# A weight sum moved from VectorE to an adding DMA issued by GpSimd, in a decoder layer's feed-forward units

## Chip, cores and metric

The kernel runs on one core of one Trainium2 chip. The metric is the device time of one execution in microseconds, as the median of several runs. Engines are named as in the profile: PE is TensorE (PEld its weight loads), DVE is VectorE, ACT is ScalarE, POOL is GpSimd, SP is SyncE, which here only issues DMAs.

## What is computed

One layer of a decoder in float32: 256 tokens (SEQ), model width 2048, feed-forward width 5504 (D_FF). The change touches the two feed-forward networks only.

```python
def swiglu_ffn(x, w_in, w_out):
    gate, up = jnp.split(x @ w_in, 2, axis=-1)
    return (jax.nn.silu(gate) * up) @ w_out

x = x + 0.5 * swiglu_ffn(rmsnorm(x, ffn1_norm[l]), ffn1_w_in[l], ffn1_w_out[l])
h = rmsnorm(x, mix_norm[l])
...   # attention mixer of two head groups, then x = x + mixed @ w_out
x = x + 0.5 * swiglu_ffn(rmsnorm(x, ffn2_norm[l]), ffn2_w_in[l], ffn2_w_out[l])
```

## The kernel before

**Products in three parts.** Every float32 operand is split into a high part (ACT copies it to float32r, tile `whi`) and a low part (DVE subtracts the high part from the original, tile `wlo`); a product is hi x hi + hi x lo + lo x hi on TensorE. The weights are split in "halves" of 128 x 1024 elements. `whi` and `wlo` have four slots, so ACT may split half h only when TensorE has used half h - 4 (`weights_used`), and TensorE takes half h when DVE has made its low part (`weights_lo`). `split` is L671 on ACT and L951 on DVE.

**Units.** `x @ w_in` is computed in 11 units of 512 columns of gate and up (`UNITS`, the last has 384). Unit 0 is plain. Units 1 to 10 compute part of the product by a scheme of Strassen's kind with seven products in place of eight: besides plain blocks of the weights (B11, B21, B22 and the plain quarters G0, G1, U0, U1) it multiplies four sums of weight blocks, T1 to T4, with four sums of activation blocks (`form_sums`) or a plain one. A unit uses 22 halves in the order T1, B11, G0, T2, B21, T3, G1, B22, T4, U (four halves: the two of U0, the two of U1), where the halves of G and U need twelve matmuls each and the others six. A "quarter of U" below is one such half.

**Sums.** DVE makes the sums of 128 x 2048 elements: T1 = B12 - B11 into the tile `tsum` (L1042), T3 = B22 - B12 in the slot of B12 (L1049), T2 = T3 + B11 in the slot of B11 (L1056) and T4 = B21 - T2 into `tsum` (L1062). Each of the sums is written out by hand at a fixed place between DVE's splits; engines work through their instructions strictly in this order. T1 and T3 of the next unit are made in the last two quarters of U of this one.

**Loads.** Each unit reads eight pieces of 1 MB from HBM into six slots of the tile `raw`. SP issues them in the order B11, B12, B22, G0, B21, G1, U0, U1; piece n takes the slot of piece n - 6 and waits until that is free (`free`), and all later pieces wait behind it. So U0 waits for the slot of B11 (which holds T2), U1 for that of B12 (T3), the next unit's B11 for that of B22, its B12 for G0's, and its B22 for B21's. Before the change the slot of B11 is free when the T4 sum is done:

```python
if i == LOAD["B11"]:
    return sums_done, 4 * ((UNITS - 1) * u + j)
last = {LOAD["B21"]: B21, LOAD["B12"]: T3, LOAD["B22"]: B22, ...
```

**GpSimd** makes a few small powers and issues the small loads: in the first network's time `bias_vector` and its copy to 128 rows of 12 KB in HBM, `bias_vectors` (L340, L342), then, once `weights_lo` has reached `OUT[0]`, the constants of the mixer.

**After the units** the product with `w_out` follows, with its own pieces, and, between the two networks, the mixer. They are as before in both kernels.

Of the kernel before, what the change touches and what calls it, by code (L numbers as in the profile page):

```python
# [91 lines left out]
def layer(nc, io, out):  # L92
# [3 lines left out]
    with ctx:  # L96
# [110 lines left out]
        def act_slot(u, c, p):  # L207
# [11 lines left out]
        silu_done, act_f_done, act_psum, act_copied, aw_hi_ready, aw_ready = (  # L219
            sem(n) for n in ("silu_done", "act_f_done", "act_psum", "act_copied", "aw_hi_ready", "aw_ready"))  # L220
        xg_ready, s_summed, s_hi, s_ready = (sem(n) for n in ("xg_ready", "s_summed", "s_hi", "s_ready"))
        sums_done, copied, w_done, gate_added, c11_done = (
            sem(n) for n in ("sums_done", "copied", "w_done", "gate_added", "c11_done"))
        sq_done, hss_ready, hms_ready, hr_ready, hsc_ready, qn_ready, qk_psum, qkT_ready, v_ready = (
# [13 lines left out]
        def _(sp):  # L238
            def free(n):
                for u in range(2):  # L240
                    if IN_P[u] <= n < OUT_P[u]:
                        j, i = (n - IN_P[u]) // 8, (n - IN_P[u]) % 8
                        if j == 0:
                            return weights_lo, IN[u] + 2 * i + 2
                        if i == LOAD["B11"]:
                            return sums_done, 4 * ((UNITS - 1) * u + j)
                        last = {LOAD["B21"]: B21, LOAD["B12"]: T3, LOAD["B22"]: B22, LOAD["G0"]: G0, LOAD["G1"]: G1, LOAD["U0"]: U0, LOAD["U1"]: U0 + 2}[i]
                        return weights_lo, unit_half(u, j) + last + 2
                    end = (QKV_P, END_P)[u]
                    if OUT_P[u] <= n < end:  # L250
                        c, q = (n - OUT_P[u]) // ACT_PAIRS, (n - OUT_P[u]) % ACT_PAIRS
                        return weights_lo, OUT[u] + FT * c + min(2 * q + 2, FT)
                return weights_lo, QKV + 2 * (n - QKV_P) + 2
# [63 lines left out]
        @block.gpsimd  # L317
        def _(pool):
            pool.memset(neg_half[:], -0.5).then_inc(small_set, 1)
            pool.memset(warm[:], 0.0).then_inc(small_set, 1)  # L320
            pool.memset(ident[:], 0.0).then_inc(ident_zero, 1)
            pool.wait_ge(ident_zero, 1)
            pool.affine_select(out=ident[:], in_=ident[:], compare_op=ALU.not_equal, fill=1.0, base=0,
                               pattern=[[-1, P]], channel_multiplier=1).then_inc(ident_ready, 1)
            pool.dma_start(table[:], io["rel_bias_table"]).then_inc(vec_loaded, 16)
            pool.dma_start(one_hot[:], io["c_one_hot"]).then_inc(vec_loaded, 16)
            pool.dma_start(vec_mask[:], io["c_vec_mask"]).then_inc(vec_loaded, 16)
            for s, name in enumerate(("mix_norm", "ffn2_norm")):
                pool.dma_start(gain_rows2[s * KT:(s + 1) * KT, :], io[name][0].rearrange("(k p) -> k p", p=P)).then_inc(gains2_loaded, 16)
            for s, name in enumerate(("q_norm_a", "k_norm_a", "q_norm_b", "k_norm_b")):  # L330
                pool.dma_start(gain_rows2[2 * KT + s:2 * KT + s + 1, :], io[name]).then_inc(gains2_loaded, 16)

            def x_power(s):
                pool.wait_ge(xms_ready, s + 1)
                pool.tensor_tensor(rstd[:, s, :], xms[:, s, :], neg_half[:, 0:TB], ALU.pow).then_inc(rstd_ready, 1)

            pool.wait_ge(small_set, 2)
            x_power(0)
            pool.wait_ge(vec_ready, 1)
            pool.dma_start(vec_dram.rearrange("a (h v) -> (a h) v", h=H_A), vec[:]).then_inc(vec_stored, 16)  # L340
            pool.wait_ge(vec_stored, 16)
            pool.dma_start(scratch, vec_dram.to_broadcast([P, H_A * VEC])).then_inc(vec_copied, 16)  # L342
            pool.wait_ge(weights_lo, OUT[0])
            pool.dma_start(wf[:], io["w_in"][0].rearrange("(k p) f -> p k f", p=P)[:, :, 6 * D_A:6 * D_A + H_B]).then_inc(f_loaded, 16)
            pool.dma_start(f_bias[:], io["forget_bias"].to_broadcast([P, H_B])).then_inc(f_loaded, 16)
            pool.dma_start(mult[:], io["c_mult"]).then_inc(mixer_loaded, 16)
            pool.dma_start(causal[:], io["c_causal"]).then_inc(mixer_loaded, 16)
            pool.dma_start(upper[:], io["c_upper"]).then_inc(mixer_loaded, 16)
            pool.wait_ge(weights_lo, QKV)
            pool.wait_ge(vec_copied, 16)  # L350
            for b in range(TB):
                src = bass.AP(tensor=scratch.tensor, offset=SEQ - 1 - b * P,
                              ap=[[H_A * VEC - 1, P], [VEC, H_A], [1, (b + 1) * P]])
                pool.dma_start(dmat[:, 0:H_A, b * P:b * P + (b + 1) * P], src).then_inc(mixer_loaded, 16)
            x_power(1)
            for m in range(2 * GROUPS):
                pool.wait_ge(hms_ready, m + 1)
                pool.tensor_tensor(hr[:], hms[:], neg_half[:].rearrange("p (b i) -> p b i", b=TB), ALU.pow).then_inc(hr_ready, 1)
            x_power(2)

        @block.tensor
        def _(pe):
# [299 lines left out]
        def _(act_e):  # L662
# [102 lines left out]
            def unit(u, j):  # L765
                Y, V, Z, X = unit_banks(j)
                base, n, w, s = unit_half(u, j), IN_P[u] + 8 * j, UNIT_W[j], j % 2
                first, w2 = (UNITS - 1) * u + j - 1, 2 * w
                act_e.wait_ge(sums_done, 4 * first + 1)
                for i in range(2):  # L770
                    split(base + T1 + i, tsum[:, i * w2:(i + 1) * w2], w2)
                loaded(n + LOAD["B11"])
# [7 lines left out]
                act_e.wait_ge(weights_used, base + B11 + 2)  # L780
                act_e.wait_ge(act_f_done, 2 * (UNITS * u + j))
                A(p1s[:, 0:w], Y[:, 0:w], ACT.Copy).then_inc(copied, 1)
                act_e.wait_ge(sums_done, 4 * first + 3)
                for i in range(2):
                    split(base + T2 + i, piece_half(n + LOAD["B11"], i, w2), w2)
                loaded(n + LOAD["B21"])
# [10 lines left out]
                for i in range(2):  # L797
                    split(base + B22 + i, piece_half(n + LOAD["B22"], i, w2), w2)
                act_copy(u, j - 1)
                act_e.wait_ge(sums_done, 4 * first + 4)  # L800
                for i in range(2):
                    split(base + T4 + i, tsum[:, i * w2:(i + 1) * w2], w2)
                loaded(n + LOAD["U0"])
                for i in range(2):
                    split(base + U0 + i, piece_half(n + LOAD["U0"], i, w2), w2)
# [140 lines left out]
        def _(dve):  # L946
# [24 lines left out]
            def form_sums(u):  # L971
# [1 line left out]
                A11, A21, A12, A22 = xg[:, 0:4, 0:P], xg[:, 0:4, P:2 * P], xg[:, 4:8, 0:P], xg[:, 4:8, P:2 * P]  # L973
                V.tensor_tensor(A22, A21, A22, ALU.add).then_inc(s_summed, 1)
                dve.wait_ge(s_summed, 4 * u + 1)
                V.tensor_tensor(A21, A11, A21, ALU.subtract).then_inc(s_summed, 1)
                V.tensor_tensor(A11, A22, A11, ALU.subtract).then_inc(s_summed, 1)
                dve.wait_ge(s_summed, 4 * u + 3)
                V.tensor_tensor(A12, A12, A11, ALU.subtract).then_inc(s_summed, 1)

            def form_splits(u):
                for f in range(4):
# [53 lines left out]
            def sum_t1(u, j):  # L1036
# [1 line left out]
                full(n + LOAD["B11"])  # L1038
                full(n + LOAD["B12"])
                if j > 1:  # L1040
                    dve.wait_ge(weights_lo, unit_half(u, j - 1) + T4 + 2)
                V.tensor_tensor(tsum[:, 0:4 * w], whole(n + LOAD["B12"], w), whole(n + LOAD["B11"], w),  # L1042
                                ALU.subtract).then_inc(sums_done, 1)

            def sum_t3(u, j):
                n, w = IN_P[u] + 8 * j, UNIT_W[j]
                full(n + LOAD["B22"])
                dve.wait_ge(sums_done, 4 * ((UNITS - 1) * u + j - 1) + 1)
                V.tensor_tensor(whole(n + LOAD["B12"], w), whole(n + LOAD["B22"], w), whole(n + LOAD["B12"], w),  # L1049
                                ALU.subtract).then_inc(sums_done, 1)  # L1050

            def sum_t2(u, j):
                n, w = IN_P[u] + 8 * j, UNIT_W[j]
                dve.wait_ge(sums_done, 4 * ((UNITS - 1) * u + j - 1) + 2)
                dve.wait_ge(weights_lo, unit_half(u, j) + B11 + 2)
                V.tensor_tensor(whole(n + LOAD["B11"], w), whole(n + LOAD["B12"], w), whole(n + LOAD["B11"], w),  # L1056
                                ALU.add).then_inc(sums_done, 1)

            def sum_t4(u, j):
                n, w = IN_P[u] + 8 * j, UNIT_W[j]  # L1060
                dve.wait_ge(sums_done, 4 * ((UNITS - 1) * u + j - 1) + 3)
                V.tensor_tensor(tsum[:, 0:4 * w], whole(n + LOAD["B21"], w), whole(n + LOAD["B11"], w),  # L1062
                                ALU.subtract).then_inc(sums_done, 1)

            def plain_unit(u):
# [25 lines left out]
            def unit(u, j):  # L1091
# [11 lines left out]
                for i in range(2):  # L1103
                    split(base + T2 + i, piece_half(n + LOAD["B11"], i, w2), w2)
                split(base + B21, piece_half(n + LOAD["B21"], 0, w2), w2)
                sum_t4(u, j)
                split(base + B21 + 1, piece_half(n + LOAD["B21"], 1, w2), w2)
                for i in range(2):
                    split(base + T3 + i, piece_half(n + LOAD["B12"], i, w2), w2)
# [4 lines left out]
                V.tensor_tensor(gset[:, s, 1, 0:w], Y[:, 0:w], gset[:, s, 1, 0:w], ALU.add).then_inc(w_done, 1)  # L1114
                for i in range(2):
                    split(base + B22 + i, piece_half(n + LOAD["B22"], i, w2), w2)
                split(base + T4, tsum[:, 0:w2], w2)
                dve.wait_ge(weights_used, base + G1 + 2)
                dve.wait_ge(w_done, first + 1)
                V.tensor_tensor(gset[:, s, 1, 0:w], X[:, 0:w], gset[:, s, 1, 0:w], ALU.add).then_inc(gate_added, 1)  # L1120
                split(base + T4 + 1, tsum[:, w2:2 * w2], w2)
                split(base + U0, piece_half(n + LOAD["U0"], 0, w2), w2)
                dve.wait_ge(weights_used, base + B22 + 2)
                dve.wait_ge(copied, 3 * first + 3)
# [208 lines left out]
```

## Time and profile before

| | before |
|---|---|
| median of 3 runs | 1793.67 us (1792.72 to 1793.70) |
| the profiled execution | 1793.74 us, its span 1791.9 us |
| granted TensorE clock, mean | 1.000 |
| PE busy | 1785.4 us |
| DVE busy | 1330.9 us |
| ACT busy | 1015.1 us |
| POOL busy | 28.6 us |
| DMA | 347.14 MB, mean 194 GB/s |

The profile is of one execution. Times in it are microseconds from the start of the span; the execution's own time is 1.8 us longer than its span. "Busy" counts an engine's instructions without waits, and matmuls overlap: one row says 0.39 us, while the next starts 0.23 us later. A line number names the line of the kernel that issued an instruction; L671 and L951 are the shared helper `split`. A load's "us to landing" runs from its issue to its semaphore.

### The profile page before, as it was taken

Reading aid. Unit: us, or ns where it says so; the run is one execution under the profiler, and the core shown is the slowest. Engines: PE = TensorE matmul, PEld = TensorE weight load, DVE = VectorE, ACT = ScalarE, POOL = GpSimd, SP = SyncE. Lnnn points to the kernel's source line nnn. Section 1 sums busy time; section 2 is a strip of 40 time slices with the busy share of each in tenths; the row PEclk is TensorE's granted clock in tenths of the full one; section 3 lists DMA queues with packets and bytes.
Section 4 is the critical chain, followed back from the end, with each engine's and each line's share of the span. In section 5 each row is a group of like instructions: output and inputs, shape, how many; then the busy total and the mean of one; then the engine's idle time right before and its main releaser. Section 6 shows DMA issues by size and latency. Waiting matters only on the chain.

```text
span 1791.9 us, 20728 instructions
## 1 busy us (share of the span) xinstructions
PE 1785.4 (100%) x8196; PEld 1491.0 (83%) x8196; DVE 1330.9 (74%) x1389; ACT 1015.1 (57%) x1244; POOL 28.6 (2%) x37
## 2 busy tenths in 40 slices
PE   9999999999999999999999999999999999999999
PEld 7888888888888888888888888888888888988887
DVE  6999999998755655565655655999999998855654
ACT  6666666666644544544545544666666666644543
POOL 1000000000000000000000000000000000000000
PEclk9999999999999999999999999999999999999999
DMA  8555555554855554445455456355555554655761
GB/s 330 189 214 218 213 188 188 188 188 167 297 196 191 187 176 176 157 149 184 154 179 164 167 185 252 126 210 191 214 217 216 216 214 154 246 189 182 229 193 53
DMA packets 153663, 347.14 MB, mean 194 GB/s; under 512 B 5840, under 2 KB 14096, under 8 KB 153440
## 3 DMA queue, kind: packets, MB, share of 16 engines
q1 hardware_dynamic: 151536, 340.28, 54.5%
q0 software_dynamic: 1168, 3.97, 0.6%
q10 hardware_dynamic: 864, 1.58, 0.2%
q8 instruction: 65, 1.06, 0.2%
q14 instruction: 30, 0.25, 0.0%
HBM read 343.70 MB, written 3.68 MB: 194 GB/s over the span
## 4 chain that ended last, share of the span: by engine, by line
PE 99%; DVE 0%; DMA 0%; ACT 0%; issue 0%; ACTq 0%; DVEq 0%
PE bank L434 10%; PE bank L436 10%; PE bank L435 10%; PE bank L500 9%; PE bank L499 9%; PE bank L501 9%; PE bank L422 7%; PE bank L424 7%; PE bank L423 7%; PE bank L372 6%; PE bank L374 6%; PE bank L373 6%; PE bank L404 1%; PE bank L393 1%; PE bank L529 0%; PE bank L576 0%
## 5 line engine op out<-in xcount | busy, mean ns | idle before, releaser
L951 DVE TENSOR_TENSOR wlo<-raw,whi 128x1024 fp32r<-128x1024 f32 (+1 forms) x692 | 824.5, 1209 | 377.7 <-ACT whi L671 373.5
L671 ACT ACTIVATE whi<-raw 128x1024 fp32r<-128x1024 f32 (+1 forms) x692 | 721.1, 1048 | 613.9 <-PE bank L501 224.3
L434 PE MATMUL bank<-whi,xs 128*128 128x512 f32 (+1 forms) x768 | 297.7, 388 | 0.3 <-DVE wlo L951 0.3
L436 PE MATMUL bank<-whi,xs 128*128 128x512 f32 (+1 forms) x768 | 295.6, 385 | 0.0
L435 PE MATMUL bank<-wlo,xs 128*128 128x512 f32 (+1 forms) x768 | 295.4, 385 | 0.0
L499 PE MATMUL bank<-whi,aw_hi 128*128 128x512 f32 x676 | 263.4, 390 | 0.0
L501 PE MATMUL bank<-whi,aw_lo 128*128 128x512 f32 x676 | 263.1, 389 | 0.0
L500 PE MATMUL bank<-wlo,aw_hi 128*128 128x512 f32 x676 | 263.0, 389 | 0.0
L434 PEld LDWEIGHTS bank<-whi,xs 128*128 128x128 f32 x768 | 144.2, 188 | 27.7 <-issue 1.2
L436 PEld LDWEIGHTS bank<-whi,xs 128*128 128x128 f32 x768 | 144.2, 188 | 27.7
L435 PEld LDWEIGHTS bank<-wlo,xs 128*128 128x128 f32 x768 | 144.3, 188 | 26.7
L372 PE MATMUL bank<-whi,xs 128*128 128x512 f32 x384 | 156.1, 406 | 0.0
L374 PE MATMUL bank<-whi,xs 128*128 128x512 f32 x384 | 150.2, 391 | 0.0
L373 PE MATMUL bank<-wlo,xs 128*128 128x512 f32 x384 | 149.7, 390 | 0.0
L501 PEld LDWEIGHTS bank<-whi,aw_lo 128*128 128x128 f32 x676 | 126.9, 188 | 26.4
L499 PEld LDWEIGHTS bank<-whi,aw_hi 128*128 128x128 f32 x676 | 126.9, 188 | 26.2
L500 PEld LDWEIGHTS bank<-wlo,aw_hi 128*128 128x128 f32 x676 | 126.9, 188 | 26.1
L671 ACT ACTIVATE whi<-tsum 128x1024 fp32r<-128x1024 f32 (+1 forms) x80 | 83.0, 1040 | 96.5 <-PE bank L436 63.8
L422 PE MATMUL bank<-whi,sf 128*128 128x512 f32 (+1 forms) x320 | 122.8, 384 | 0.0
L424 PE MATMUL bank<-whi,sf 128*128 128x512 f32 (+1 forms) x320 | 122.8, 384 | 0.0
L423 PE MATMUL bank<-wlo,sf 128*128 128x512 f32 (+1 forms) x320 | 122.8, 384 | 0.0
L951 DVE TENSOR_TENSOR wlo<-tsum,whi 128x1024 fp32r<-128x1024 f32 (+1 forms) x80 | 94.0, 1197 | 25.7 <-ACT whi L671 25.7
(168 smaller groups left out, 1973.5 us busy)
## 6 DMA issues: line engine op xcount, KB each, us to landing
raw<-ffn_w_in SPq DMA_DIRECT2D x159, 1024.0 KB, 7.1
raw<-ffn_w_out SPq DMA_DIRECT2D x84, 1024.0 KB, 5.5
raw<-w_in SPq DMA_DIRECT2D x48, 1024.0 KB, 5.0
raw<-w_out SPq DMA_DIRECT2D x16, 1024.0 KB, 4.9
raw<-ffn_w_in SPq DMA_DIRECT2D x16, 768.0 KB, 4.5
x<-x SPq DMA_DIRECT2D x4, 512.0 KB, 8.9
raw<-ffn_w_out SPq DMA_DIRECT2D x4, 512.0 KB, 3.8
bias_vectors<-bias_vector POOLq DMA_DIRECT2D x1, 1536.0 KB, 9.3
```

The costliest lines, as they stand in the source:

```text
L372: mm(banks[b][:, 0:w], stationary[:, k, 0, tok], hi, start=k == 0, stop=False, skip_group_check=True)
L373: mm(banks[b][:, 0:w], stationary[:, k, 0, tok], lo, start=False, stop=False, skip_group_check=True)
L374: last = mm(banks[b][:, 0:w], stationary[:, k, 1, tok], hi, start=False, stop=k == k_total - 1, skip_group_check=True)
L422: mm(bank_out[:, 0:w], st_hi, hi, start=start and i == 0 and k == 0, stop=False, skip_group_check=True)
L434: mm(banks[b][:, 0:w], xs[:, k + i, 0, tok], hi, start=starts[b] and k + i == 0, stop=False, skip_group_check=True)
L435: mm(banks[b][:, 0:w], xs[:, k + i, 0, tok], lo, start=False, stop=False, skip_group_check=True)
L436: last = mm(banks[b][:, 0:w], xs[:, k + i, 1, tok], hi, start=False, stop=k + i == last_k, skip_group_check=True)
L499: mm(banks[i][b][:], st_hi, hi, start=k == 0, stop=False, skip_group_check=True)
L500: mm(banks[i][b][:], st_hi, lo, start=False, stop=False, skip_group_check=True)
L501: last = mm(banks[i][b][:], st_lo, hi, start=False, stop=k == FT - 1, skip_group_check=True)
L671: A(whi[:, h % SLOTS, 0:n_el], src, ACT.Copy).then_inc(weights_hi, 1)
L951: V.tensor_tensor(wlo[:, h % SLOTS, 0:n_el], src, whi[:, h % SLOTS, 0:n_el].bitcast(f32), ALU.subtract).then_inc(weights_lo, 1)
```

## The change

In units 1 to 10 of both networks VectorE's T4 sum is gone. GpSimd issues a DMA with `accum_op=ALU.add` from the slot of B11, which holds T2, into the slot of B21, which so becomes T4. It waits for the T2 sum and for the low part of B21. A DMA can add and not subtract, so the signs of T2 and T3 are turned (and in `form_sums` those of the activation sums multiplied with them). The slot of B11 becomes free when this transfer has landed, the slot of B21 after the split of T4, and the sum of the next T1 into `tsum` waits only for the split of T1.

```diff
@@ loads (SP)
                         if i == LOAD["B11"]:
-                            return sums_done, 4 * ((UNITS - 1) * u + j)
-                        last = {LOAD["B21"]: B21, ...
+                            return t4_summed, 16 * ((UNITS - 1) * u + j)
+                        last = {LOAD["B21"]: T4, ...
@@ GpSimd
+            def sum_t4(u, j):
+                n, w, first = IN_P[u] + 8 * j, UNIT_W[j], (UNITS - 1) * u + j - 1
+                b11, b21 = raw_slot(n + LOAD["B11"]), raw_slot(n + LOAD["B21"])
+                pool.wait_ge(sums_done, 3 * first + 3)
+                pool.wait_ge(weights_lo, unit_half(u, j) + B21 + 2)
+                pool.dma_start(raw[:, b21, 0:4 * w], raw[:, b11, 0:4 * w], accum_op=ALU.add).then_inc(t4_summed, 16)
+
+            for j in range(1, UNITS):
+                sum_t4(0, j)
             pool.wait_ge(weights_lo, OUT[0])
...
             x_power(2)
+            for j in range(1, UNITS):
+                sum_t4(1, j)
@@ ScalarE, unit
-                act_e.wait_ge(sums_done, 4 * first + 4)
-                for i in range(2):
-                    split(base + T4 + i, tsum[:, i * w2:(i + 1) * w2], w2)
+                act_e.wait_ge(t4_summed, 16 * (first + 1))
+                for i in range(2):
+                    split(base + T4 + i, piece_half(n + LOAD["B21"], i, w2), w2)
@@ VectorE, form_sums
-                V.tensor_tensor(A21, A11, A21, ALU.subtract).then_inc(s_summed, 1)
-                V.tensor_tensor(A11, A22, A11, ALU.subtract).then_inc(s_summed, 1)
+                V.tensor_tensor(A21, A21, A11, ALU.subtract).then_inc(s_summed, 1)
+                V.tensor_tensor(A11, A11, A22, ALU.subtract).then_inc(s_summed, 1)
                 dve.wait_ge(s_summed, 4 * u + 3)
-                V.tensor_tensor(A12, A12, A11, ALU.subtract).then_inc(s_summed, 1)
+                V.tensor_tensor(A12, A12, A11, ALU.add).then_inc(s_summed, 1)
@@ VectorE, sum_t1, sum_t3, sum_t2
-                    dve.wait_ge(weights_lo, unit_half(u, j - 1) + T4 + 2)
+                    dve.wait_ge(weights_lo, unit_half(u, j - 1) + T1 + 2)
...
-                V.tensor_tensor(whole(n + LOAD["B12"], w), whole(n + LOAD["B22"], w), whole(n + LOAD["B12"], w),
+                V.tensor_tensor(whole(n + LOAD["B12"], w), whole(n + LOAD["B12"], w), whole(n + LOAD["B22"], w),
                                 ALU.subtract).then_inc(sums_done, 1)
...
                 V.tensor_tensor(whole(n + LOAD["B11"], w), whole(n + LOAD["B12"], w), whole(n + LOAD["B11"], w),
-                                ALU.add).then_inc(sums_done, 1)
-
-            def sum_t4(u, j):
-                n, w = IN_P[u] + 8 * j, UNIT_W[j]
-                dve.wait_ge(sums_done, 4 * ((UNITS - 1) * u + j - 1) + 3)
-                V.tensor_tensor(tsum[:, 0:4 * w], whole(n + LOAD["B21"], w), whole(n + LOAD["B11"], w),
                                 ALU.subtract).then_inc(sums_done, 1)
@@ VectorE, unit
                 split(base + B21, piece_half(n + LOAD["B21"], 0, w2), w2)
-                sum_t4(u, j)
                 split(base + B21 + 1, piece_half(n + LOAD["B21"], 1, w2), w2)
...
-                split(base + T4, tsum[:, 0:w2], w2)
+                split(base + T4, piece_half(n + LOAD["B21"], 0, w2), w2)
...
-                split(base + T4 + 1, tsum[:, w2:2 * w2], w2)
+                split(base + T4 + 1, piece_half(n + LOAD["B21"], 1, w2), w2)
```

`sums_done` now counts three sums a unit, and the waits on it are renumbered.

## Rows read from the trace of the kernel before

**Rows 1.** The page's first part: busy time, share of the span, instructions.
```profile
PE 1785.4 (100%) x8196; PEld 1491.0 (83%) x8196; DVE 1330.9 (74%) x1389; ACT 1015.1 (57%) x1244; POOL 28.6 (2%) x37
```

**Rows 2.** Busy time by stretches; then granted clock, DMA share, GB/s.
```profile
1189.00:1550.00 361.00, 361.00 (x1667) 304.20 (x1666) 330.94 (x285) 233.94 (x261) 0.00 (x0) 1.00 0.54 195
...
262.60:304.30 41.70, 41.70 (x189) 34.61 (x188) 38.41 (x33) 26.80 (x29) 0.00 (x0) 1.00 0.55 200
273.00:280.60 7.60, 7.60 (x36) 6.27 (x35) 7.46 (x7) 4.67 (x5) 0.00 (x0) 1.00 0.00 0
```

**Rows 3.** Instructions of DVE in order: start, us, line, operation, count, idle before.
```profile
278.28 2.28 DVE L1062 TENSOR_TENSOR tsum<-raw 128x2048 f32<-128x2048 f32 x1
280.48 2.36 DVE L951 TENSOR_TENSOR wlo<-raw,whi 128x1024 fp32r<-128x1024 f32 x2
...
293.40 1.23 DVE L951 TENSOR_TENSOR wlo<-tsum,whi 128x1024 fp32r<-128x1024 f32 x1 [0.40 <-ACT whi L671]
...
298.98 2.28 DVE L1042 TENSOR_TENSOR tsum<-raw 128x2048 f32<-128x2048 f32 x1
301.18 1.22 DVE L951 TENSOR_TENSOR wlo<-raw,whi 128x1024 fp32r<-128x1024 f32 x1
...
307.06 1.22 DVE L951 TENSOR_TENSOR wlo<-raw,whi 128x1024 fp32r<-128x1024 f32 x1 [0.19 <-ACT whi L671]
308.62 0.75 DVE L1004 SCALAR_TENSOR_TENSOR gset<-bank,rstd,gset 128x512 f32<-128x512 f32 x1 [0.34 <-PE bank L436]
...
310.68 2.35 DVE L951 TENSOR_TENSOR wlo<-raw,whi 128x1024 fp32r<-128x1024 f32 x2
```

**Rows 4.** PE's first matmul of T4, of U, of B11's second half (next unit).
```profile
294.82 0.39 PE L422 MATMUL bank<-whi,xs 128*128 128x512 f32 x1
...
297.54 0.39 PE L434 MATMUL bank<-whi,xs 128*128 128x512 f32 x1
...
312.50 0.39 PE L422 MATMUL bank<-whi,xs 128*128 128x512 f32 x1
```

**Rows 5.** The T4 sums of DVE: duration in ns min/median/max, forms.
```profile
L1062 DVE TENSOR_TENSOR tsum<-raw x20: 1753/2284/2289, 69.7 to 1530.6; 128x2048 f32<-128x2048 f32 x18, 128x1536 f32<-128x1536 f32 x2
```

**Rows 6.** ACT in order: high part of B21's second half, of T4, of U0.
```profile
278.70 1.06 ACT L671 ACTIVATE whi<-raw 128x1024 fp32r<-128x1024 f32 x1 [1.60 <-PE bank L436]
...
289.64 1.06 ACT L671 ACTIVATE whi<-tsum 128x1024 fp32r<-128x1024 f32 x1 [0.75 <-PE bank L436]
...
293.72 1.06 ACT L671 ACTIVATE whi<-raw 128x1024 fp32r<-128x1024 f32 x1 [0.36 <-PE bank L424]
```

**Rows 7.** SP's waits for the T4 sum: us in total, times, longest.
```profile
SPq L261 <- DVE tsum L1062: 389.8, 20, 20.6
```

**Rows 8.** Loads and landing: U0 alone; B11', B12', B22' together.
```profile
L261 SPq DMA_DIRECT2D raw<-ffn_w_in x1: 368/368/368, 280.6 to 280.6; - x1
...
DMA to landing us min/median/max: 5.0/5.0/5.0
...
L261 SPq DMA_DIRECT2D raw<-ffn_w_in x2: 367/437/507, 289.9 to 290.3; - x2
...
L261 SPq DMA_DIRECT2D raw<-ffn_w_in x3: 367/505/507, 289.9 to 290.8; - x3
...
DMA to landing us min/median/max: 5.0/7.2/9.2
```

**Rows 9.** DMA issues of GpSimd: KB each, us to landing.
```profile
dmat<-bias_vectors POOLq DMA_DIRECT2D x1, 1024.0 KB, 9.8
...
bias_vector<-vec POOLq DMA_DIRECT2D x1, 12.0 KB, 1.7
```

**Rows 10.** The 128-row transfer's issue; queues in 52 to 55.2, then from 55.2.
```profile
52.03 0.55 POOL L342 DMA_DIRECT2D bias_vectors<-bias_vector  x1 [1.46 <-DMA bias_vector<-vec]
...
q1 hardware_dynamic: 479, 0.98, 92.4%
...
q0 software_dynamic: 144, 1.57, 74.5%
```

More of the change, by code:

```diff
@@ L221, in layer @@
         xg_ready, s_summed, s_hi, s_ready = (sem(n) for n in ("xg_ready", "s_summed", "s_hi", "s_ready"))
+        t4_summed = sem("t4_summed")
         sums_done, copied, w_done, gate_added, c11_done = (
@@ L245, in free @@
                         if i == LOAD["B11"]:
-                            return sums_done, 4 * ((UNITS - 1) * u + j)
-                        last = {LOAD["B21"]: B21, LOAD["B12"]: T3, LOAD["B22"]: B22, LOAD["G0"]: G0, LOAD["G1"]: G1, LOAD["U0"]: U0, LOAD["U1"]: U0 + 2}[i]
+                            return t4_summed, 16 * ((UNITS - 1) * u + j)
+                        last = {LOAD["B21"]: T4, LOAD["B12"]: T3, LOAD["B22"]: B22, LOAD["G0"]: G0, LOAD["G1"]: G1, LOAD["U0"]: U0, LOAD["U1"]: U0 + 2}[i]
                         return weights_lo, unit_half(u, j) + last + 2
@@ L768, in unit @@
                 first, w2 = (UNITS - 1) * u + j - 1, 2 * w
-                act_e.wait_ge(sums_done, 4 * first + 1)
+                act_e.wait_ge(sums_done, 3 * first + 1)
                 for i in range(2):
@@ L782, in unit @@
                 A(p1s[:, 0:w], Y[:, 0:w], ACT.Copy).then_inc(copied, 1)
-                act_e.wait_ge(sums_done, 4 * first + 3)
+                act_e.wait_ge(sums_done, 3 * first + 3)
                 for i in range(2):
@@ L1047, in sum_t3 @@
                 full(n + LOAD["B22"])
-                dve.wait_ge(sums_done, 4 * ((UNITS - 1) * u + j - 1) + 1)
-                V.tensor_tensor(whole(n + LOAD["B12"], w), whole(n + LOAD["B22"], w), whole(n + LOAD["B12"], w),
+                dve.wait_ge(sums_done, 3 * ((UNITS - 1) * u + j - 1) + 1)
+                V.tensor_tensor(whole(n + LOAD["B12"], w), whole(n + LOAD["B12"], w), whole(n + LOAD["B22"], w),
                                 ALU.subtract).then_inc(sums_done, 1)
@@ L1053, in sum_t2 @@
                 n, w = IN_P[u] + 8 * j, UNIT_W[j]
-                dve.wait_ge(sums_done, 4 * ((UNITS - 1) * u + j - 1) + 2)
+                dve.wait_ge(sums_done, 3 * ((UNITS - 1) * u + j - 1) + 2)
                 dve.wait_ge(weights_lo, unit_half(u, j) + B11 + 2)
                 V.tensor_tensor(whole(n + LOAD["B11"], w), whole(n + LOAD["B12"], w), whole(n + LOAD["B11"], w),
-                                ALU.add).then_inc(sums_done, 1)
-            def sum_t4(u, j):
-                n, w = IN_P[u] + 8 * j, UNIT_W[j]
-                dve.wait_ge(sums_done, 4 * ((UNITS - 1) * u + j - 1) + 3)
-                V.tensor_tensor(tsum[:, 0:4 * w], whole(n + LOAD["B21"], w), whole(n + LOAD["B11"], w),
                                 ALU.subtract).then_inc(sums_done, 1)
```

## The prediction

> **What bounds the kernel now.** I read the page's first part, then the table by stretches, then one unit of the first feed-forward layer instruction by instruction on every engine. The first part [rows 1] shows TensorE busy 1785.4 of 1791.9 us, VectorE 74%, GpSimd 2%. By stretches [rows 2] TensorE is busy 361.0 of 361.0 us where the units of the second layer lie and 41.70 of 41.70 in the unit under study, at full clock. So nothing taken off VectorE inside the units can shorten the kernel; what can happen there is that TensorE starts to wait.
>
> A unit lasts 41.7 us [rows 2]. The matmul rows [rows 4] give the deadlines of the unit under study: T4 is needed at 294.82, the first quarter of U at 297.54. T4's 12 matmuls took 2.72 us, and each quarter of U has 12: so the last one is needed at 297.54 + 3 x 2.72 = 305.70, and the second half of the next unit's B11 at 312.50. ("Next" things carry a prime below.) On DVE, from the T1' sum at 298.98 on, one instruction follows the next with only two small waits, 0.19 and 0.34 us, up to the low part of the second half of B11', which starts at 310.68, takes 1.22 us (first of two), and so ends at 311.90 [rows 3]. TensorE wants it at 312.50: 0.60 us to spare. That is the narrowest place I found. DVE may therefore be late at the T1' sum by 0.19 + 0.34 + 0.60 = 1.13 us before TensorE waits.
>
> **The change part by part.**
>
> *Removed: the VectorE sums.* 20 of them, 18 of 2.284 us and the two of the narrow last units 1.753 us [rows 5], 44.6 us in all. They are hidden behind TensorE, so this gives 0. In the unit, DVE does the sum from 278.28 to 280.56 and then the low part of the second half of B21, from 280.48 [rows 3]; ACT delivers that half's high part at 278.70 + 1.06 = 279.76, held by TensorE [rows 6]. So with the sum gone that low part ends near 279.8 + 1.23 = 281.03 instead of 281.7: a start of the new work only 0.7 us earlier than before.
>
> *Turned signs.* The same subtractions and additions at the same shapes; 0. The T1' sum now waits only for T1's split, long past; 0.
>
> *Added: 20 adding transfers of 1 MB on GpSimd's queue.* GpSimd waits for the T2 sum (five instructions before the T4 sum on DVE, long done) and for the low part of B21, so it issues at 281.06. Queued behind it on GpSimd in layer 1 are five constant loads that wait for the end of the units anyway, and in layer 2 nothing: 0. When it issues, nothing is in flight: the data engines moved 0 GB/s from 273.0 to 280.6 [rows 2], and the loads behind it are the very ones that wait for it. Call D its time from issue to landing. No adding transfer stands in the trace, so I bound D.
> Below: a plain 1 MB load issued by SP with the engines idle lands in 5.0 us [rows 8]; loads queued one behind another land 2.6 and 2.5 us apart (289.9 + 5.0 = 294.9, 290.3 + 7.2 = 297.5, 290.8 + 9.2 = 300.0) [rows 8], so 2.55 us is data and 2.4 us fixed.
> GpSimd's queue starts later: of the transfer of 128 rows of 12 KB issued at 52.03 [rows 10] no packet had moved by 55.2, when only SP's queue appears, and in the window from 55.2 on it is there [rows 10]: 3.2 us. With data at copy speed D would be 3.2 + 2.55 = 5.75.
> But an adding transfer has to read both the T2 slot and the B21 slot for each result, and I take the reads as the limit: 2 x 2.55 = 5.1. D = 3.2 + 5.1 = 8.3, and 0.2 for the completion, which the rows don't separate: 8.5 us. I take this value, since it is nearest to a row in kind (same queue, 128 rows). Above: the 1 MB gather-like load of the mixer on this queue landed in 9.8 us among other traffic [rows 9]; and if the adder runs at half the pace of the doubled reads, 3.2 + 10.2 = 13.4.
>
> The Trainium skill, Collectives: The Full Stack, in "Why ReduceScatter is half of AllGather", says that an add in the data engines costs no cycles of its own and halves the rate only because two sources are read. By that rule the sum would be the one made here with 8.5 (1828 us), without it that of 13.4 (1906 us, below). No row of this trace shows an add, so it stays unconfirmed.
>
> *What hangs on D: the T4 split.* ACT takes T4 at 289.64 [rows 6]; TensorE needs it at 294.82, less 1.06 + 1.23 for the two parts: until 292.5. From 281.06 that is D = 11.4. At 8.5 it costs 0.
>
> *The slot of B11.* It was free when the T4 sum ended (280.56) and U0's load was issued at once, at 280.6; SP spent 389.8 us in 20 waits for exactly this [rows 7]. Now U0's load waits for the landing: issue at I = 281.06 + D + 0.03. It lands at I + 5.0 = 294.6 for D = 8.5; ACT wants it at 293.72, but TensorE only needs the low part by 297.54, so it may land until 295.2 (D = 9.1). Costs 0 by itself.
>
> *What is late next.* This is the term that decides. Behind U0 SP's queue holds U1, B11', B12'. Before, U0 and U1 were out of the way when B11' was issued at 289.9 with the engines free; B12' landed at 297.5 and the T1' sum, which needs it, started at 298.98 [rows 3, 8]. Now U0's load is issued at 289.59 and four loads run one after the other: B12' lands at I + 5.0 + 3 x 2.55 = I + 12.65 = 302.2. The T1' sum starts then: 302.2 - 298.98 = 3.3 us late. Behind it on DVE stand the last quarter of U (ends at 302.40 + 3.3 = 305.7, needed at 305.70: just), the T3' sum, T1', B11'. 3.26 less the 1.13 of slack is 2.1 us of TensorE waiting, in general 281.09 + D + 12.65 - 298.98 - 1.13 = D - 6.4 us.
> All later times of the unit that are tied to TensorE move by the same 2.1 us, the next adding transfer too, since DVE, freed of its sum, regains its lateness before B21 (1.4 us of room: B21's first half ended at 278.36, 279.76 is held by TensorE [rows 3, 6]). So it recurs and neither grows nor heals.
>
> *The slot of B21.* It now frees after T4's second low part, 293.40 + 1.23 = 294.63 [rows 3], instead of at 281.7, so B22' and all behind it on SP's queue can't be issued before that; before it was issued at 290.8 [rows 8]. With the engines idle it would land at 299.7, and behind B12' it lands at 304.8; the T3' sum wanted it at 302.3, behind the split of 301.18 [rows 3], and wants it at 305.6 in the forecast. Costs 0 either way; the cover is DVE's own lateness, 0.8 us of it.
>
> *How often.* Each layer has ten such units; the last has no successor with sums, and the ninth's successor has 384 columns: its two loads are 0.64 us shorter each, its two sums 0.53 each, its splits together an estimated 0.8, against 1.0 us by which its deadline is nearer; that is 2.1 us less 1.28 + 1.06 + 0.8 - 1.0 = 2.1, so nothing. So 8 per layer, 16 in all: 16 x 2.1 = 34 us.
>
> **Sum.** The profiled execution took 1793.74 us (its span 1791.9, 1.8 around it), 0.07 above the median of the runs: 1793.7 + 34 = 1828 us.
>
> **The rivals.**
> *Quick start.* The 12 KB transfer on the same queue landed in 1.7 us [rows 9]. If 128 rows start as fast, D = 1.7 + 5.1 = 6.8, the wait is 0.4 a unit, 7 us in all: 1801. For it: the 3.2 us come from one transfer amid traffic. Against: that one has 16 times the rows.
> The Trainium skill, DMA: Bandwidth & Descriptors, section "Anatomy of one DMA — SWDGE (gpsimd) path", puts a transfer on this queue at 2.0 us plus its bytes at 436 GB/s; with bytes read twice that is an estimate of 6.8, where the first-packet delay in this trace speaks for more.
> *Hidden anyway.* At copy speed D is 5.75, or 5.0 as on SP's queue; both are under 6.4, TensorE never waits: 1794. For it: everything else in the unit has room. Against: two reads.
> *Adder slow.* D = 13.4: the wait is 7.0 a unit through the same chain (the T4 and U0 deadlines are passed as well, by 2.0 and 4.3 us, but they lie on the same chain and don't add): 16 x 7.0 = 112, so 1906. For it: no row shows what the adder does. Against: nothing but that the reads alone explain a cost.
> *Faster.* Its one mechanism: VectorE's 44.6 us less lets a wait of TensorE's inside the units vanish. It decides only if there is one; the unit under study and the second layer's stretch show none. If the rest of the 6.5 us idle [rows 1] had such waits, all of it at most: 1787. A transfer that lands early changes nothing on TensorE.
> That the change doesn't do what it says is not open: one form of T4 or the other must feed the matmuls.
>
> **How the numbers follow.** D between 7.5 and 10 (forecast, 1811 to 1852): 0.43. D from 6.6 to 7.5 (quick start): 0.12. D above 10: 0.24, half of it above 12. D below 6.6, no change: 0.18. Faster: 0.03. 0.2%, 3.6 us, is about what these runs can tell from nothing; it is 0.2 us a unit, D = 6.6. So slower 0.79, same 0.18, faster 0.03. The range runs from 1793 (no change) to D = 12, 16 x 5.6 = 90: 1884; it leaves out 0.12 above and 0.03 below. The forecast's own range is 1811 to 1852.
>
> **What would show it.** The adding transfer's time to landing near 8.5 us; SP's wait for U0's slot near 28 us each; DVE idle some 3.3 us before most T1 sums, ended by a load; TensorE waiting some 2 us before the second half of B11 and nowhere else, at a unit period near 43.8; VectorE's busy time down by 44.6. I'm wrong if D is under 6.4, if loads run behind one another faster than 2.55 us, if TensorE waits at T4 or U0 instead, or if the wait heals in the next unit.

## The result and the profile after

The changed kernel took 1825.67 us (median, 1824.61 to 1826.41), the kernel before 1793.68 us in the same session: ratio 1.0178, 95% interval 1.0165 to 1.0191, 32 us slower. The forecast was 1828, its own range 1811 to 1852. Two single executions of kernels below were in a slow state (4302.60 us with the two half transfers, 2235.94 with the load held less) and are left out of the medians given.

First the page's first part, then the table by stretches (columns: busy us and count for PE, PEld, DVE, ACT, POOL; granted clock, DMA share, GB/s), which answer to [rows 1, 2]:

```profile
span 1822.8 us, 20748 instructions
PE 1795.1 (98%) x8196; PEld 1487.5 (82%) x8196; DVE 1288.3 (71%) x1369; ACT 1011.3 (55%) x1244; POOL 45.8 (3%) x57
```
```profile
70.00:450.00 380.00, 366.90 (x1621) 296.78 (x1620) 310.54 (x266) 229.90 (x252) 7.77 (x9) 1.00 0.63 217
1190.00:1540.00 350.00, 342.79 (x1532) 281.17 (x1531) 295.46 (x254) 216.71 (x236) 6.82 (x8) 1.00 0.64 224
```

VectorE's busy time fell by 42.6 us (forecast 44.6; its other rows together took 2.0 longer) and TensorE gained idle time where it had none: 13.1 us in 380 of layer 1, 7.2 in 350 of layer 2, still at full clock. (That is less than the time lost: around a wait TensorE's rows overlap less and read longer, 0.47 and 0.50 us below against 0.39, so PE's busy total rose by 9.7 us as well.)

DVE in the unit that corresponds to [rows 3], in order:

```profile
293.42 2.59 DVE L964 TENSOR_TENSOR wlo<-raw,whi 128x1024 fp32r<-128x1024 f32 x2 [1.23 <-ACT whi L684]
...
316.07 2.29 DVE L1055 TENSOR_TENSOR tsum<-raw 128x2048 f32<-128x2048 f32 x1 [3.40 <-DMA raw<-ffn_w_in]
318.28 1.22 DVE L964 TENSOR_TENSOR wlo<-raw,whi 128x1024 fp32r<-128x1024 f32 x1
...
325.02 0.74 DVE L1017 SCALAR_TENSOR_TENSOR gset<-bank,rstd,gset 128x512 f32<-128x512 f32 x1
...
327.07 2.35 DVE L964 TENSOR_TENSOR wlo<-raw,whi 128x1024 fp32r<-128x1024 f32 x2
```

The second half of B21 is split from 293.42 on, held by ScalarE as forecast, and its low part ends at 294.64. The T1' sum (now L1055) then waits 3.40 us for a load, where nothing waited before; the two small waits that followed it have vanished (no bracket at 325.02). Between this low part and the T1' sum lies the new work. GpSimd's row in order of time, then the time from issue to landing of this one transfer:

```profile
295.18 0.85 POOL L350 DMA_DIRECT2D raw<-raw  x1 [43.52 <-DVE wlo L964]
```
```profile
DMA to landing us min/median/max: 6.8/6.8/6.8
```

SP's loads U0 and U1, issued together, and B12' (duration of the issue in ns, first and last start; then us to landing):

```profile
L262 SPq DMA_DIRECT2D raw<-ffn_w_in x2: 368/438/508, 302.0 to 302.5; - x2
DMA to landing us min/median/max: 4.9/6.0/7.0
...
L262 SPq DMA_DIRECT2D raw<-ffn_w_in x1: 627/627/627, 303.9 to 303.9; - x1
DMA to landing us min/median/max: 12.1/12.1/12.1
```

GpSimd issues at 295.18 and the transfer lands 6.8 us later, at 302.0. At that moment SP issues U0, then U1, and B12' as the fourth at 303.9: it lands at 303.9 + 12.1 = 316.0, and the T1' sum starts at 316.07. SP's waits and TensorE's own rows of the same unit (start, us, line, idle before):

```profile
SPq L262 <- DMA raw<-raw: 528.0, 20, 30.2
```
```profile
322.98 0.47 PE L435 MATMUL bank<-whi,sf 128*128 128x512 f32 x1 [0.40 <-DVE wlo L964]
...
328.34 0.50 PE L435 MATMUL bank<-whi,xs 128*128 128x512 f32 x1 [1.00 <-DVE wlo L964]
```

SP's 20 waits for the slot of B11 grew from 19.5 us each [rows 7] to 26.4 (forecast: near 28), and TensorE waits at T1' and at the second half of B11'.

The two layers don't pay alike. GpSimd's power ahead of layer 2's units marks the border; it began at 1133.15 in the kernel before, and here:

```profile
1153.27 1.60 POOL L336 TENSOR_TENSOR rstd<-xms,neg_half 128x2 f32<-128x2 f32 x1 [145.47 <-DVE xms L1003]
```

So layer 1 pays 20.1 us and layer 2 the rest of the 30.9 us by which the span grew, 10.8. The border of each kernel below is this same row. Compared matmul by matmul with the kernel before, TensorE falls further behind in eight units of each layer, by 2.5 us a unit on average in layer 1 and 1.3 in layer 2, and not in the ninth (the last costs 0.5 in layer 2).

### The profile page after: what moved, and what is told of

It is laid out like the page before. It is cut to its first block, busy times and chain, and to the rows that moved or that the text cites. A ratio compares the mean times of both kernels' runs of the same rounds, so it can differ in the third digit from the quotient of the medians.

```text
span 1822.8 us, 20748 instructions
## 1 busy us (share of the span) xinstructions
PE 1795.1 (98%) x8196; PEld 1487.5 (82%) x8196; DVE 1288.3 (71%) x1369; ACT 1011.3 (55%) x1244; POOL 45.8 (3%) x57
## 3 DMA queue, kind: packets, MB, share of 16 engines
q8 instruction: 65, 1.06, 0.2%
## 4 chain that ended last, share of the span: by engine, by line
PE 73%; DVE 12%; DMA 10%; issue 4%; ACT 0%; SPq 0%; DVEq 0%; POOLq 0%; ACTq 0%
PE bank L513 8%; PE bank L514 8%; PE bank L512 8%; DMA raw<-ffn_w_in 8%; PE bank L385 6%; PE bank L387 6%; PE bank L386 6%; DVE wlo L964 6%; PE bank L447 5%; PE bank L449 5%; PE bank L448 5%; PE bank L435 4%; PE bank L437 3%; PE bank L436 3%; DVE tsum L1055 2%
## 5 line engine op out<-in xcount | busy, mean ns | idle before, releaser
L964 DVE TENSOR_TENSOR wlo<-raw,whi 128x1024 fp32r<-128x1024 f32 (+1 forms) x732 | 872.7, 1208 | 437.0 <-ACT whi L684 432.3
L684 ACT ACTIVATE whi<-raw 128x1024 fp32r<-128x1024 f32 (+1 forms) x732 | 761.3, 1047 | 643.2 <-PE bank L514 224.4
L447 PE MATMUL bank<-whi,xs 128*128 128x512 f32 (+1 forms) x768 | 298.8, 389 | 3.4 <-DVE wlo L964 3.2
L449 PE MATMUL bank<-whi,xs 128*128 128x512 f32 (+1 forms) x768 | 295.6, 385 | 0.0
L448 PE MATMUL bank<-wlo,xs 128*128 128x512 f32 (+1 forms) x768 | 295.4, 385 | 0.0
L435 PE MATMUL bank<-whi,xs 128*128 128x512 f32 (+1 forms) x240 | 94.2, 392 | 14.9 <-DVE wlo L964 14.9
L436 PE MATMUL bank<-wlo,xs 128*128 128x512 f32 (+1 forms) x240 | 92.2, 384 | 0.0
```

The source lines that it names most:

```text
L435: mm(bank_out[:, 0:w], st_hi, hi, start=start and i == 0 and k == 0, stop=False, skip_group_check=True)
L436: mm(bank_out[:, 0:w], st_hi, lo, start=False, stop=False, skip_group_check=True)
L447: mm(banks[b][:, 0:w], xs[:, k + i, 0, tok], hi, start=starts[b] and k + i == 0, stop=False, skip_group_check=True)
L448: mm(banks[b][:, 0:w], xs[:, k + i, 0, tok], lo, start=False, stop=False, skip_group_check=True)
L449: last = mm(banks[b][:, 0:w], xs[:, k + i, 1, tok], hi, start=False, stop=k + i == last_k, skip_group_check=True)
L684: A(whi[:, h % SLOTS, 0:n_el], src, ACT.Copy).then_inc(weights_hi, 1)
```

## The experiments

**The slot of B11 freed early.** The adding transfer stays, but T2 is written into `tsum`, which is free since T1's split, and the slot of B11 is free when that sum is done. The next T1 sum waits for the transfer instead.

```diff
-                            return t4_summed, 16 * ((UNITS - 1) * u + j)
+                            return sums_done, 3 * ((UNITS - 1) * u + j)
...
-                pool.dma_start(raw[:, b21, 0:4 * w], raw[:, b11, 0:4 * w], accum_op=ALU.add).then_inc(t4_summed, 16)
+                pool.dma_start(raw[:, b21, 0:4 * w], tsum[:, 0:4 * w], accum_op=ALU.add).then_inc(t4_summed, 16)
...
-                    dve.wait_ge(weights_lo, unit_half(u, j - 1) + T1 + 2)
+                    dve.wait_ge(t4_summed, 16 * ((UNITS - 1) * u + j - 1))
...
-                V.tensor_tensor(whole(n + LOAD["B11"], w), whole(n + LOAD["B12"], w), whole(n + LOAD["B11"], w),
+                V.tensor_tensor(tsum[:, 0:4 * w], whole(n + LOAD["B12"], w), whole(n + LOAD["B11"], w),
```
(T2's splits on both engines read `tsum`.)

> The adding transfer stays, but T2 is made in tsum, so the slot of B11 is free when the T2 sum is done (near 273.5 in the unit of the profile before) and U0's load no longer waits for the transfer. Theory A (the cost is the row U0, U1, B11', B12' on SP's queue behind the landing, which delays the T1' sum): B12' lands as before, 1794 us, within 3. Rival B (the late slot of B21, which holds B22' and all behind it): unchanged by this edit, 1826. Rival C (the transfer itself: its traffic, or T4 arriving late at ScalarE): 1826 as well.

Measured: 1793.62 us, ratio 1.0000 (0.9990 to 1.0009). Its page, then the landing of its 20 transfers:

```profile
span 1791.9 us, 20748 instructions
PE 1785.4 (100%) x8196; PEld 1490.9 (83%) x8196; DVE 1290.9 (72%) x1369; ACT 1015.4 (57%) x1244; POOL 45.9 (3%) x57
```
```profile
DMA to landing us min/median/max: 6.7/7.9/9.1
```

The transfers are there (and even slower, 7.9 us in the median, beside loads), the slot of B21 is as late as in the change, the signs are turned, 20 sums are gone from VectorE: all of that together costs and gives nothing. The cost of the change hangs on how late the slot of B11 is freed.

**Two transfers of half the size.**

```diff
-                pool.wait_ge(weights_lo, unit_half(u, j) + B21 + 2)
-                pool.dma_start(raw[:, b21, 0:4 * w], raw[:, b11, 0:4 * w], accum_op=ALU.add).then_inc(t4_summed, 16)
+                for i in range(2):
+                    c = slice(2 * w * i, 2 * w * (i + 1))
+                    pool.wait_ge(weights_lo, unit_half(u, j) + B21 + 1 + i)
+                    pool.dma_start(raw[:, b21, c], raw[:, b11, c], accum_op=ALU.add).then_inc(t4_summed, 16)
```

> The transfer is cut in two of 512 KB, each issued when its half of B21 is split. The second has half the data, 2.5 us in place of 5.1, so U0's load is issued some 2.5 us earlier, near 285.6 in the clock of the unit before. Theory A: threshold for that is about 287.1, so no wait is left or a few tenths where a data engine is held up: 1794 to 1800 us. Rival B: 1826. Rival C with a cost per transfer: over 1826.

Measured: 1795.86 us, ratio 1.0012 (1.0003 to 1.0022). Each half landed in 4.5 us (median) in place of 6.9; the loss is gone but for 2.1 us.

**A plain copy in place of the add.**

```diff
-pool.dma_start(raw[:, b21, 0:4 * w], raw[:, b11, 0:4 * w], accum_op=ALU.add)
+pool.dma_start(raw[:, b21, 0:4 * w], raw[:, b11, 0:4 * w])
```

> The same transfer as a plain copy of T2 over B21; the addition is left out. If the doubled reads are the reason for the transfer's 6.9 us, it lands in 6.9 - 2.5 = 4.4 us, and by theory A TensorE hardly waits: 1794 to 1800 us. If the add itself were costless or the time came from GpSimd's queue, it would still land in 6.9 and the time stay 1826. Rival B: 1826.

Measured: 1794.01 us, ratio 1.0003 (0.9993 to 1.0012). The DMA issues (KB each, us to landing), of the changed kernel and then of this one:

```profile
raw<-raw POOLq DMA_DIRECT2D x18, 1024.0 KB, 6.9
```
```profile
raw<-raw POOLq DMA_DIRECT2D x18, 1024.0 KB, 4.5
```

The add costs 2.4 us over the copy, about one more pass of 1 MB at 2.55 us [rows 8]: what I had charged for reading two sources. (No run tells the second read from the addition itself.)

**The kernel before, with U0's load held.** No adding transfer at all.

```diff
-                            return sums_done, 4 * ((UNITS - 1) * u + j)
+                            return weights_lo, unit_half(u, j) + B22 + 1
```

> The kernel before, with VectorE's T4 sum and no adding transfer, but U0's load held until the low part of B22's first half is done (288.7 in the unit of the profile before, where the change puts its issue near 288.5). Theory A: the same waits as with the change, 1.2 to 2.5 us a unit, 1815 to 1830 us. Rivals B and C (slot of B21, traffic, T4 late): none of them is there, 1794.

Measured: 1824.57 us, ratio 1.0173 (1.0156 to 1.0190), the change's time within 1.1 us; layer 1 pays 17.0 and layer 2 13.6 us. The late load alone is enough for the whole loss.

**The same, held 2.2 us less** (`G1 + 2` in place of `B22 + 1`).

> The kernel before with U0's load held until the low part of G1's second half is done, 286.5 in the unit of its profile. Theory A with its threshold near 286.7 to 287.1: 1794 to 1799 us, against 1824.6 when held until 288.7. If holding U0's load costs something at any length: well over 1800.

Measured: 1795.09 us, ratio 1.0008 (0.9998 to 1.0018). 2.2 us of delay separate 1.4 us of loss from 30.9: there is a threshold. By an estimate from these two, 29.5 us over 16 units are 1.8 us a unit, which puts it near 286.9, between the two releases (286.5 and 288.7, as times of the unit in the profile before).

**The transfer one half later.**

```diff
-                pool.wait_ge(weights_lo, unit_half(u, j) + B21 + 2)
+                pool.wait_ge(weights_lo, unit_half(u, j) + B21 + 3)
```

> The adding transfer waits for one more low part (first half of T3), 1.36 us later. Theory A says that every microsecond of delay is one of waiting in 16 to 18 units: 1826 + 22 = 1848 us, plus or minus 4. If the T4 split or the slot of B21 set the wait, the delay would be taken up by their slack (over 2 us before T4 is wanted): 1826.

Measured: 1849.68 us, 24.0 over the changed kernel; layer 1 pays 12.0 us more, layer 2 13.1. In total that is one for one in 18 units (18 x 1.36 = 24.5). Unit by unit it is uneven: from one adding transfer to the next, layer 1's units grew by 0.2 to 2.5 us over those of the change.

**Half of U1's load left out.**

```diff
-                        piece(n + LOAD["U1"], w_in[:, 4:8, up], 4, w)
+                        piece(n + LOAD["U1"], w_in[:, 4:6, up], 2, w)
```

> The changed kernel with U1's load cut to half its bytes; the second half of that piece is left out and stale data are used. Theory A: four loads run in a row from the landing to B12', each 2.57 us; with 1.28 us less, B12' lands that much earlier and each of 16 to 18 waits shrinks by 1.1 to 1.3 us: 1826 - 20 = 1806 us, plus or minus 3. If U0's own lateness or the T4 split made TensorE wait: 1826.

Measured: 1801.14 us. A load that nobody was late for (U1), made shorter, takes back 24.5 of 32 us: the waits belong to the row of loads. It is 2 us beyond the expected margin. Layer 1 gained 14.7 us, of which 1.0 lies ahead of the units (the first power row stands at 43.42 in place of 44.39), so 13.7 in eight units, 1.7 each, more than the 1.3 us of load; layer 2 gained 7.6. The excess lies in every second unit of layer 1, which gained 1.8 to 2.4 us, the others 1.2 to 1.4. In the change's second unit B12' landed 14.0 us after the adding transfer had, and a 16 KB block of instructions fell into its last stretch, 18.4 us after that transfer's issue (such blocks are the subject further down). With the shorter load the block comes 18.4 us after the issue again, but B12' has already landed, at 18.3 and 11.3 us after the adding transfer.

**VectorE's sum in the slot of B21.** The signs and slots of the change, but the sum is VectorE's, after the second half of B21.

```diff
                 split(base + B21 + 1, piece_half(n + LOAD["B21"], 1, w2), w2)
+                dve.wait_ge(sums_done, 3 * ((UNITS - 1) * u + j - 1) + 3)
+                dve.wait_ge(weights_lo, unit_half(u, j) + B21 + 2)
+                V.tensor_tensor(whole(n + LOAD["B21"], w), whole(n + LOAD["B21"], w), whole(n + LOAD["B11"], w),
+                                ALU.add).then_inc(t4_summed, 1)
```

> The changed kernel with its signs, its T4 in the slot of B21 and that slot's late release, but the sum is VectorE's again, after the second half of B21. Theory A: the slot of B11 is free near 283.4, U0's load early enough, 1794 us. Rival B (slot of B21 free only after T4's split): 1826. Turned signs: 1826 if they cost anything.

Measured: 1810.95 us, ratio 1.0097 (1.0082 to 1.0112). All three expectations miss. Its DVE and PE rows say why:

```profile
284.40 1.23 DVE L953 TENSOR_TENSOR wlo<-raw,whi 128x1024 fp32r<-128x1024 f32 x1 [1.43 <-ACT whi L673]
285.73 2.29 DVE L1105 TENSOR_TENSOR raw<-raw 128x2048 f32<-128x2048 f32 x1
287.94 2.35 DVE L953 TENSOR_TENSOR wlo<-raw,whi 128x1024 fp32r<-128x1024 f32 x2
```
```profile
289.30 0.47 PE L424 MATMUL bank<-whi,sf 128*128 128x512 f32 x1 [0.60 <-DVE wlo L953]
```

The split ahead of the sum is held by ScalarE until 284.40, so the sum of 2.29 us pushes the first half of T3 to 287.94 + 1.2 = 289.2, and TensorE waits for it at 289.30: a new wait at T3 of 0.60 us here, with a loss of 0.86 us a unit on average (17.2 us over 20 units). It has nothing to do with slots. Before, the sum stood ahead of that split, in the time in which VectorE would have waited for ScalarE anyway.

**Why layer 1 pays twice as much.** The queue of instruction blocks (q8) shows one packet of 16 KB on one data engine beside the other traffic; here in two windows of the changed kernel, 167 to 169 and 313.3 to 314.6:

```profile
q0 software_dynamic: 37, 0.18, 44.9%
q8 instruction: 1, 0.02, 3.0%
```
```profile
q1 hardware_dynamic: 251, 0.49, 99.7%
q8 instruction: 1, 0.02, 4.8%
```

The first falls into an adding transfer, the second into the last stretch of B12', which landed at 316.0 where 302.0 + 12.65 is 314.7. It is so unit by unit: of layer 1's transfers in units that pay, five landed in 7.2 to 8.6 us and had an instruction packet begin 3.4 to 6.9 us after their issue; the other three landed in 6.9 and had a block begin 18.3 to 18.4 us after it, and there B12' came 1.3 to 1.4 us late (one of the five had that too). The landing of the adding transfers by layer (windows 70 to 440 and 1180 to 1530):

```profile
DMA to landing us min/median/max: 6.8/7.5/8.6
```
```profile
DMA to landing us min/median/max: 6.8/6.8/7.0
```

Two of the units of layer 2 that pay have no instruction packet in their transfer and row of loads; here is one of them, from its adding transfer to the next:

```profile
1266.77 0.85 POOL L350 DMA_DIRECT2D raw<-raw  x1 [42.19 <-DVE wlo L964]
1309.47 0.85 POOL L350 DMA_DIRECT2D raw<-raw  x1 [41.86 <-DVE wlo L964]
```

It lasts 42.70 us, as does the other (1439.18 to 1481.88), against 41.7 before: without a block a unit loses 1.0 us.

To move these blocks against the units, 44 matmuls (88 instructions with their weight loads) were added at the start, to the changed kernel and to the kernel before.

```diff
-            wake(16)
+            wake(60)
```

> In the changed kernel the units of layer 1 lasted 43.4 to 44.7 us, those of layer 2 42.7 to 43.6. Theory D: in layer 1 a 16 KB block of instructions (0.9 to 1.3 us on one data engine, every 28 us) falls in turn on the adding transfer and on the load of B12', in layer 2 mostly beside them. 44 more matmuls at the start shift the blocks by some 10 us against the units, to about 6 us before the transfer, 7 and 24 us after its start: layer 1's units should fall to 42.7 to 43.6, some 8 us less in all, less the 2 to 5 us that the added matmuls cost at the start (told by the kernel before with the same addition); layer 2's may change either way by up to 1.3 us a unit. Rival: layer 1 is slower for its data or its place, and the units stay at 44.2.

> The kernel before with the same 44 added matmuls at the start, to know their own cost: 2 to 5 us over 1793.7, and units of 41.7 us in both layers.

Measured: 1828.58 us with the change, 1797.22 us without (span 3.8 us longer, all of it at the start). The first power row and the border row of the two, changed kernel first:

```profile
46.48 1.56 POOL L336 TENSOR_TENSOR rstd<-xms,neg_half 128x2 f32<-128x2 f32 x1 [40.06 <-DVE xms L1003]
...
1148.31 1.60 POOL L336 TENSOR_TENSOR rstd<-xms,neg_half 128x2 f32<-128x2 f32 x1 [145.47 <-DVE xms L1003]
```
```profile
48.21 1.56 POOL L335 TENSOR_TENSOR rstd<-xms,neg_half 128x2 f32<-128x2 f32 x1 [41.80 <-DVE xms L990]
...
1136.94 1.60 POOL L335 TENSOR_TENSOR rstd<-xms,neg_half 128x2 f32<-128x2 f32 x1 [145.47 <-DVE xms L990]
```

The added matmuls delay the first power row by 2.1 us with the change and by 3.8 without (it stood at 44.39 in both kernels), so the layers are counted from that row. The change now costs layer 1 13.1 us (1101.83 less 1088.73) in place of 20.1, and layer 2 18.3 in place of 10.8. Same data, same code in the units, only the position in the instruction stream moved. So the two layers differ by where the blocks fall. That the sum stayed nearly the same, 30.9 and 31.4 us, is chance as far as these runs show. The Trainium skill, Runtime: NRT & Kernel Launch, section "Instruction fetch mechanics", says that an engine's instructions are refilled in blocks of 16 KB, 256 instructions; 88 of them are a third of a block, and that is how the shift was sized. The trace agrees: queue q8 carries 65 packets and 1.06 MB in the whole changed kernel, and TensorE's 2 x 8196 instructions make 64 blocks of 256.

## Why the prediction was right, and what in it was not

- **TensorE bounds the units, less work on VectorE gives 0; the signs, GpSimd's queue and the slot of B21 cost 0.** Right: with the slot of B11 freed early all of them are present and the time is 1793.62.
- **The chain: landing, U0, U1, B11', B12', T1' sum, and TensorE at the second half of B11'.** Right, and shown link by link: its start alone (U0 held) gives 1824.6; 1.36 us more delay costs 24.0 us; a shorter load in its middle gives 24.5 back; under the threshold 1.4 us is lost. The waits of 3.40 us on DVE and 1.00 on PE stand where they were forecast. Besides, TensorE waits 0.40 us at T1', which the forecast excluded ("nowhere else"): T1's low part was done 2.7 us ahead of its need before (305.7 against 308.42), which 3.4 us of lateness use up.
- **D, issue to landing.** Mis-sized: 6.9 us in the median, not 8.5. The second pass over the data was right in size: 6.9 against 4.5 for the copy. With the rule of the Trainium skill, Collectives: The Full Stack, "Why ReduceScatter is half of AllGather", that an add costs only the second read, the trace agrees in size. Wrong was the start of 3.2 us, taken from a transfer amid other traffic. No packet had moved 1.3 us after the issue, in the window from 295.1 to 296.5:

```profile
DMA packets 0, 0.00 MB, mean 0 GB/s; under 512 B 0, under 2 KB 0, under 8 KB 0
```

  By 297.0 sixteen packets had, so the first came some 1.4 us after the issue. A copy pass of 2.55 us with the add's 2.4 leaves about 1.9 us of 6.8 for start and end together. The trace's packet records say the same: the first packet begins 1.42 to 1.53 us after the issue in all 20 transfers, the last mostly ends 0.3 us before the landing, and a packet of 8 KB takes 0.63 us with the add where the copy takes 0.32. The quick-start rival had D right, 6.8, and by the prediction's own division D between 6.6 and 7.5 was that rival's case (0.12), with 1801 us. The estimate by the Trainium skill, DMA: Bandwidth & Descriptors, "Anatomy of one DMA — SWDGE (gpsimd) path", was 6.8 too, and the trace agrees.
- **The issue at once after B21's low part.** Mis-sized: GpSimd issues at 295.18, 0.54 us after 294.64, where SP follows its release in 0.03. This gives a third of the error in D (1.6 to 1.7 us) back.
- **Loads in a row at 2.55 us.** Right where no instruction block falls among them: with the transfer's landing at 1273.6 in layer 2 the T1' sum starts at 1286.29, 12.7 us later (forecast: 12.65 and 0.03). In layer 1 the unit shown needs 14.0 us, 1.3 more, where an instruction block holds up one data engine. The prediction had no such term; it put the blocks at nothing without naming them.
- **2.1 us a unit, 16 units.** The count was right: eight units pay in each layer and the ninth doesn't. The sum is 34 against 31 to 32 us, but as a mean of unlike layers. By the corrected terms the clean case is 0.54 + 6.8 + 12.7 = 20.0 us from the split of B21 to the T1' sum, less 17.95 before (298.98 - 281.03) and less the slack of 1.13: 1.0 us a unit, which is what the two units without a block lost. Eight such units are 8 us; layer 2's 10.8 and layer 1's 20.1 have the blocks on top. The prediction came out right in its chain and place. In size it is right by luck: 1.2 us too much from the split to the landing (8.53 against 7.34) and the term left out nearly cancel. With only the first put right it would have said 16 x 0.94 = 15 us, 1809, below its own range.

Not settled: the last 2.1 us of the two half transfers, which fit a held-up data engine (in the profiled execution two units lose time, and in both an instruction packet falls into the second half transfer) but were not tested; and why a packet of 0.9 to 1.4 us on one data engine makes a transfer up to 1.7 us later.

## What to carry to other kernels

When a buffer's release is handed from a compute engine to a transfer, follow the issue queue past the load that now waits: here that load itself had time to spare, and the third behind it was late. If the last reader of a buffer gets slower, let it read from elsewhere (T2 in `tsum`) or cut it so that half is done early; these took back 32 and 30 of 32 us. But neither beat the kernel before: work taken off an engine that isn't the bound is worth nothing until it is used.

## What the runs showed of the hardware that was not expected

- An adding transfer of 1 MB within SBUF takes 6.8 us alone on the data engines, a copy of the same shape 4.5.
- GpSimd's DMA row starts 0.54 to 0.61 us after the low part that it waits for, in all 20 transfers, and takes 0.85; SP's load follows the landing in 0.02 to 0.03 and its row takes 0.37 (up to 0.63 for the later ones of a row of loads).
- A 16 KB instruction block on one data engine lengthens a 16-engine transfer that it meets: adding transfers of 8.6 us in place of 6.8, a load landing 1.3 us late. Where a chain of transfers is critical, the position of the blocks counts: with 88 more instructions at the start of the program the loss in layer 1 fell by 7.0 us and that in layer 2 rose by 7.5.
